# A two-layer transformer block: row-summing exponential on ScalarE, and the output projection's last two columns by token halves

## What is computed

```python
h = rms_norm(x, g[0]);  x = x + 0.5 * rms_norm(swiglu(h, w_ffn_in[layer, 0], w_ffn_out[layer, 0]), g[1])
h = rms_norm(x, g[2])
qa, ka, va, qh, fh, ih, gh = split(h @ w_in[layer])
ya = rms_norm(sliding_window_sink_attention(qa, ka, va, sinks, rel_bias), attn_out_gain)
yh = hgrn2_mixer(qh, fh, ih, gh, lower_bounds, hgrn_norm_gain)
x = x + rms_norm(concatenate([ya, yh]) @ w_out[layer], g[3])
h = rms_norm(x, g[4]);  x = x + 0.5 * rms_norm(swiglu(h, w_ffn_in[layer, 1], w_ffn_out[layer, 1]), g[5])
# in the attention, 8 heads, windows of 128 keys, one sink logit a head:
m = maximum(max(logits), sink);  p = exp(logits - m)
probs = p / (sum(p) + exp(sink - m))
```

## Time and profile before

| | |
|---|---|
| median of 3 runs | 1989.49 us |
| the profiled execution | 1988.35 us |
| its span | 1986.6 us |
| PE busy | 1926.0 us, 97% |
| DVE busy | 747.1 us, 38% |
| ACT busy | 676.0 us, 34% |
| POOL busy | 871.9 us, 44% |
| mean granted TensorE clock | 0.995 |

### The profile page before, as it was taken

One profiled execution on the slowest core, in us unless ns is written; L12 is line 12 of the kernel. 1 busy time (PEld: TensorE's weight loads), 2 busy tenths in 40 slices (PEclk: granted clock), 3 DMA queues, 4 the chain that ended last, 5 costly groups with the idle time before them and its releaser, 6 DMA issues.

```text
span 1986.6 us, 29215 instructions
## 1 busy us (share of the span) xinstructions
PE 1926.0 (97%) x11226; PEld 1581.1 (80%) x11226; DVE 747.1 (38%) x1118; ACT 676.0 (34%) x904; POOL 871.9 (44%) x407
## 2 busy tenths in 40 slices
PE   6999999999999999999999999999999999999998
PEld 5888888877777788888888888888777778888887
DVE  4322210377775522210162222105777663222103
ACT  4332322443444323232253232224333453323221
POOL 5444445442235544345363444455322354444452
PEclk9999999999999999999999999999999999999999
DMA  5323233221112232323322323232211223232331
GB/s 173 106 85 106 89 101 115 93 84 61 54 65 85 85 106 86 104 95 109 104 85 95 100 90 106 95 112 83 89 50 53 75 75 106 95 103 87 106 106 64
DMA packets 54040, 182.81 MB, mean 92 GB/s; under 512 B 6696, under 2 KB 10312, under 8 KB 53960
## 3 DMA queue, kind: packets, MB, share of 16 engines
q1 hardware_dynamic: 53960, 181.65, 28.0%
HBM read 179.14 MB, written 2.49 MB: 91 GB/s over the span
## 4 chain that ended last, share of the span: by engine, by line
PE 86%; DVE 5%; issue 3%; POOL 2%; POOLq 2%; ACT 1%; DVEq 1%; DMA 0%; SPq 0%; ACTq 0%
PE bank L685 25%; PE bank L687 24%; PE bank L686 24%; PE pair L825 2%; DVE SM L1184 2%; PE bank L703 2%; PE bank L704 2%; POOLq L378 1%; PE bank L711 1%; POOL WLO L369 1%; PE pair L685 1%; PE pair L686 1%; PE pair L687 1%; DVE TREE_F L1172 1%; DVE QE L1174 1%
## 5 line engine op out<-in xcount | busy, mean ns | idle before, releaser
L369 POOL TENSOR_TENSOR WLO<-RAW,WHI 128x1024 fp32r<-128x1024 f32 (+1 forms) x336 | 794.9, 2386 | 1062.3 <-ACT WHI L426 1061.8
L686 PE MATMUL bank<-HLO,WHI 128*128 128x512 f32 x1616 | 630.2, 390 | 0.0
L685 PE MATMUL bank<-HHI,WHI 128*128 128x512 f32 x1568 | 621.4, 396 | 2.0 <-DVE TMP L982 1.0
L687 PE MATMUL bank<-HHI,WLO 128*128 128x512 f32 x1568 | 611.4, 390 | 0.0
L426 ACT ACTIVATE WHI<-RAW 128x1024 fp32r<-128x1024 f32 (+1 forms) x336 | 337.0, 1037 | 73.5 <-PE bank L687 55.1
L686 PEld LDWEIGHTS bank<-HLO,WHI 128*128 128x128 f32 x1616 | 303.6, 188 | 60.8 <-issue 0.5
L685 PEld LDWEIGHTS bank<-HHI,WHI 128*128 128x128 f32 x1568 | 294.3, 188 | 68.8 <-issue 3.2
L687 PEld LDWEIGHTS bank<-HHI,WLO 128*128 128x128 f32 x1568 | 294.4, 188 | 62.2
L685 PE MATMUL bank<-UHI,WHI 128*128 128x512 f32 x616 | 242.9, 394 | 0.0
L687 PE MATMUL bank<-UHI,WLO 128*128 128x512 f32 x616 | 241.6, 392 | 0.0
L686 PE MATMUL bank<-ULO,WHI 128*128 128x512 f32 x616 | 239.2, 388 | 0.0
(11 more groups left out here) (183 smaller groups left out, 1843.4 us busy)
## 6 DMA issues: line engine op xcount, KB each, us to landing
RAW<-stream SPq DMA_DIRECT2D x336, 512.0 KB, 3.7
X<-xT SPq DMA_DIRECT2D x4, 512.0 KB, 9.0
yT<-X SPq DMA_DIRECT2D x16, 128.0 KB, 1.8
bias<-rel_scratch SPq DMA_DIRECT2D x4, 128.0 KB
rel_scratch<-SM SPq DMA_DIRECT2D x1, 382.0 KB
mask_sb<-masks SPq DMA_DIRECT2D x1, 256.0 KB, 10.7
par<-sinks SPq DMA_DIRECT2D x4, 2.0 KB, 4.3
par<-params SPq DMA_DIRECT2D x1, 60.0 KB, 2.2
```

Source lines behind the costliest of these rows:

```text
L369: pool.tensor_tensor(WLO[:, n, 0:cols], RAW[:, n, 0:cols], WHI[:, n, 0:cols], ALU.subtract)\
L685: pe.matmul(dst, WHI[:, slot, lhs], rhs_hi, start=first, stop=False)
L686: pe.matmul(dst, WHI[:, slot, lhs], rhs_lo, start=False, stop=False)
L687: ins = pe.matmul(dst, WLO[:, slot, lhs], rhs_hi, start=False, stop=last)
```

## The change

The softmax: DVE makes the negated maximum with one instruction (the sinks are negated once, in the setup) and the sinks' differences; it no longer subtracts over the logits nor sums the rows. ACT runs one exponential for each of the 8 blocks of 128 keys, with the negated maximum as its bias and the row sum as its second output, and one more for the sinks. `next_take(0)` moves from in front of the wait for the exponential to behind `p_ready`. The output projection: columns 6 and 7 both run by halves (banks 2 and 5 for the first halves, 3 and 6 for the second); SS holds six columns, and two squares are added at each end; ACT's order becomes `high` 0, split, square of column 6, `high` 1, 2, square of column 7, `high` 3, split, root. DVE copies the second half of column 6 in its pre stage, behind the batch of part 3. The semaphore counts change through `half_count`; the FFNs' own ends keep their order.

```diff
--- before.py
+++ after.py
@@ -99,6 +99,11 @@
 BATCHES = [[0], [1, 2], [3], [4], [5, 6], [7], [8, 9], [10], [11]]
 TEMPS = [(5, 0), (5, 1), (7, 1), (5, 0), (5, 1), (6, 1), (5, 0), (4, 0), 6, 5, 4, 6]
 LAST = 3 * DEPTH - 1
+
+
+def half_count(g):
+
+    return g + (g + 1) // 3
 
 
 def parts_of(g):
@@ -503,16 +508,40 @@
                             elif not (last and b == 3 and n >= per - (1 if g < LAST else 2)):
                                 split_hi(L, c0 + b * per + n + 2, i, 4 * per)
                         q = Q_POST[s] + b
-                        if not (last and b == 3):
+                        if not (last and b >= (2 if k_outer else 3)):
                             act.wait_ge(proj_free, L * LAYER_JOBS + i * 4 + (j0 + b + 1 + PROJ_BANKS))
                             act.wait_ge(sq_free, L * LAYER_SQ + i * 4 + (q + 1))
                             act.activation(SQ[:, q % 2, :], Y[:, i * 4 + b, :], ACT.Square).then_inc(sq_done, 1)
                 body(0, False)
                 body(1, True)
 
+                first, second = HALVES_OF
+                if k_outer:
+                    q = Q_POST[s] + KT - 2
+                    for n, b in enumerate((2, 5)):
+                        act.wait_ge(half_full, half_count(g) + n + 1)
+                        act.wait_ge(sq_free, L * LAYER_SQ + (q + n + 1))
+                        act.activation(SQ[:, (q + n) % 2, first], bank[b][:, 0:HALF], ACT.Square).then_inc(half_sq, 1)
+                    act.wait_ge(half_sum, g + 1)
+                    rsqrt_mean(bank[7][:, first], bank[4][:, 0:HALF], D_MODEL).then_inc(post_r, 1)
+
+                    def second_square(n, b):
+                        act.wait_ge(w_used, L * LAYER_CHUNKS + (c0 + KT - 2 + n + 1 + SPLIT_SLOTS))
+                        act.activation(SQ[:, (q + n) % 2, second], bank[b][:, 0:HALF], ACT.Square).then_inc(sq_done, 1)
+
+                    high(g + 1, 0)
+                    split_hi(L, c0 + KT + 1)
+                    second_square(0, 3)
+                    high(g + 1, 1)
+                    high(g + 1, 2)
+                    second_square(1, 6)
+                    high(g + 1, 3)
+                    split_hi(L, c0 + KT + 2)
+                    act.wait_ge(sq_free, L * LAYER_SQ + (q + 2 + SQ_SLOTS))
+                    rsqrt_mean(bank[7][:, second], bank[4][:, 0:HALF], D_MODEL).then_inc(post_r, 1)
+                    return
                 q = Q_POST[s] + KT - 1
-                first, second = HALVES_OF
-                act.wait_ge(half_full, g + 1)
+                act.wait_ge(half_full, half_count(g) + 1)
                 act.wait_ge(sq_free, L * LAYER_SQ + (q + 1))
                 act.activation(SQ[:, q % 2, first], bank[5][:, 0:HALF], ACT.Square).then_inc(half_sq, 1)
                 act.wait_ge(half_sum, g + 1)
@@ -606,7 +635,10 @@
                     if t > 0:
                         head_norm(t - 1)
                     act.wait_ge(logit_ready, it + 1)
-                    act.activation(S[:], S[:], ACT.Exp).then_inc(exp_ready, 1)
+                    for n in range(8):
+                        act.activation(Slog[:, n, :], Slog[:, n, :], ACT.Exp, bias=small[:, 0, n:n + 1],
+                                       accum_out=small[:, 1, n:n + 1])
+                    act.activation(Ssink, Ssink, ACT.Exp).then_inc(exp_ready, 1)
                     ahead(0)
                     for half in range(2):
                         act.wait_ge(pt_full, it * 2 + (half + 1))
@@ -735,6 +767,30 @@
                         total(SS[:], 4, (sq_free, L * LAYER_SQ + (Q_PRE[s] + KT + SQ_SLOTS)), pre_sum)
                 return at
 
+            def out_end(L, c, hi, lo, tiles):
+
+                g = L * 3 + 1
+                first, second = HALVES_OF
+                own = slice(0, HALF)
+                q = Q_POST[1] + KT - 2
+                for n, b in enumerate((2, 5)):
+                    chunk(L, c + n, tiles, hi, lo, b, signal=half_full, w=own, rhs_w=first)
+                pe.wait_ge(sq_free, L * LAYER_SQ + (q + SQ_SLOTS))
+                pe.matmul(bank[4][:, own], ones[:], SS[:, first], start=True, stop=False)
+                chunk(L, c, tiles[:3], hi, lo, 3, ready=False, done=False, w=own, rhs_w=second)
+                for n in range(2):
+                    pe.wait_ge(half_sq, half_count(g) + n + 1)
+                    ins = pe.matmul(bank[4][:, own], ones[:], SQ[:, (q + n) % 2, first], start=False, stop=n == 1)
+                ins.then_inc(half_sum, 1)
+                chunk(L, c, tiles[3:], hi, lo, 3, ready=False, w=own, rhs_w=second)
+                chunk(L, c + 1, tiles, hi, lo, 6, ready=False, w=own, rhs_w=second)
+                pe.wait_ge(post_r, 2 * g + 1)
+                pe.matmul(bank[4][:, own], ones[:], SS[:, second], start=True, stop=False)
+                for n in range(2):
+                    pe.wait_ge(sq_done, L * LAYER_SQ + (q + n + 1))
+                    ins = pe.matmul(bank[4][:, own], ones[:], SQ[:, (q + n) % 2, second], start=False, stop=n == 1)
+                ins.then_inc(sq_free, 2)
+
             def down(L, s, c0, j0, width, hi, lo, h=None, m0=0):
 
                 g = L * 3 + s
@@ -745,13 +801,17 @@
                 def tiles_of(n):
                     return [(k - n * TILES, k, k == 0, k == width - 1) for k in range(n * TILES, min(width, (n + 1) * TILES))]
 
-                for m in range(m0, KT - 1):
+                pair_end = s == 1
+                for m in range(m0, KT - 2 if pair_end else KT - 1):
                     bank_free(L, j0 + m)
                     for n in range(per):
                         wait = h is not None and m == 0
                         chunk(L, c0 + m * per + n, tiles_of(n), hi, lo, m % 4,
                               h_sem=h[0] if wait else None, h_value=h[1] if wait else None)
                 bank_free(L, j0 + KT - 1)
+                if pair_end:
+                    out_end(L, c0 + KT - 2, hi, lo, tiles_of(0))
+                    return
                 c_last = c0 + (KT - 1) * per
                 for n in range(per):
                     chunk(L, c_last + n, tiles_of(n), hi, lo, 5, done=n == per - 1, signal=half_full, w=own, rhs_w=first)
@@ -762,16 +822,13 @@
                     tiles = tiles_of(n)
                     if n == 0:
                         chunk(L, c_last, tiles[:3], hi, lo, 6, ready=False, done=False, w=own, rhs_w=second)
-                        pe.wait_ge(half_sq, g + 1)
+                        pe.wait_ge(half_sq, half_count(g) + 1)
                         pe.matmul(bank[4][:, own], ones[:], SQ[:, q % 2, first], start=False, stop=True).then_inc(half_sum, 1)
                         tiles = tiles[3:]
-                    if n == per - 1 and per > 1:
+                    if n == per - 1:
                         pe.wait_ge(post_r, 2 * g + 1)
                         pe.matmul(bank[4][:, own], ones[:], SS[:, second], start=True, stop=False)
                     chunk(L, c_last + n, tiles, hi, lo, 6, ready=False, w=own, rhs_w=second)
-                if per == 1:
-                    pe.wait_ge(post_r, 2 * g + 1)
-                    pe.matmul(bank[4][:, own], ones[:], SS[:, second], start=True, stop=False)
                 pe.wait_ge(sq_done, L * LAYER_SQ + (q + 1))
                 pe.matmul(bank[4][:, own], ones[:], SQ[:, q % 2, second], start=False, stop=True).then_inc(sq_free, 1)
 
@@ -1021,6 +1078,9 @@
                     for p in batch:
                         k, w = parts[p]
                         dve.tensor_tensor(X[:, k, w], X[:, k, w], temp(p), ALU.add).then_inc(x_ready, 1)
+                    if batch[-1] == SPLIT_TILES - 1 and s == 2:
+                        dve.wait_ge(sq_done, L * LAYER_SQ + (Q_POST[1] + KT - 1))
+                        dve.tensor_copy(Y[:, KT - 2, HALVES_OF[1]], bank[3][:, 0:HALF]).then_inc(proj_free, 1)
                     if batch[-1] == 2 * SPLIT_TILES - 2:
                         take_last()
                 gain = par[:, L, P_GAIN + 2 * s * KT:]
@@ -1033,12 +1093,16 @@
 
             def down(L, s, c0, j0, per, k_outer=False):
 
-                for m in range(KT - 1):
+                for m in range(KT - 2 if k_outer else KT - 1):
                     c = c0 + 3 if k_outer and m < 4 else c0 + m * per + per - 1
                     take(L, c, Y[:, m, :], bank[m % 4][:], scale=False,
                          four=(2, m) if k_outer and m < 4 else None).then_inc(proj_free, 1)
                     add_square(L, Q_POST[s], m)
-                dve.wait_ge(half_sq, L * 3 + (s + 1))
+                g = L * 3 + s
+                dve.wait_ge(half_sq, half_count(g) + 1)
+                if k_outer:
+                    dve.tensor_copy(Y[:, KT - 2, HALVES_OF[0]], bank[2][:, 0:HALF])
+                    dve.wait_ge(half_sq, half_count(g) + 2)
                 dve.tensor_copy(Y[:, KT - 1, HALVES_OF[0]], bank[5][:, 0:HALF])
                 dve.drain()
 
@@ -1143,23 +1207,19 @@
                     top = small[:, 0, :]
```

(11 more changed lines are left out.)

## The result

The changed kernel takes 1973.51 us (median of 4 runs, 1973.25 to 1973.74), the kernel before 1988.99 beside it: 15.5 us less, a ratio of 0.9923 with a 95% interval from 0.9911 to 0.9935. The forecast was 1980.3 with 1978.0 to 1986.0 as its range. The direction was right and the gain was taken too small by 6 to 7 us, outside the range. The profiled execution took 1973.74 us, its span 1971.7, at a granted clock of 0.998.

A forecast was written before the change was run, and what follows sets the result against it. TensorE, 97% busy, was taken to bound the kernel, with gains only where it stands still. Output projection 6.7 plus softmax 2.5 made 9.2 us off: 1979.15 for the profiled execution, 1980.3 as median, range 1978.0 to 1986.0.

The forecast's parts named there:

- What bounds the kernel: Whole kernel: TensorE is busy 97% of 1986.6 us, so only its stalls, at most some 60 us, can be won.
- Part 1: Output projection's end: running columns 6 and 7 by halves brings the second root earlier, 3.1 + 3.6 = 6.7 us.
- the stage hangs on the second root: Output projection: the stage's end moves with the second root, HLO ending 22.4 us behind it, not with TensorE's restart.
- (c): Output projection: second root stays behind in ACT's queue, so less is won; 1982.3 to 1984.5 us, chance 0.10.
- (d): Output projection: POOL's additions and HLO fall apart, HLO runs nearer its unheld time; 1976 to 1978.9 us, chance 0.05.
- Part 2: Softmax: shorter wait ahead of the transposes, 0.75 us in each of 2 first heads, 0.17 in 6 others, 2.5 us.
- floor of 0.35: Softmax's transposes: TensorE needs about 0.35 us to go over to small tiles even where nothing is late.
- The idle time as the price: Softmax's transposes: recorded idle time, 1.41 and 0.52 us, less 0.35 taken as winnable: 1.06 and 0.17 a head.
- The 0.3 that a first head was to lose: First head's softmax: WLO runs until 434.3 and holds `widen(0)`, needed by the scores at 434.73; 0.3 us lost.
- price X: Softmax on ACT: time of one 128-element exponential with its row sum, taken as 0.45 us, between 0.28 and 0.74.
- (a): Softmax: price X between 0.575 and 0.68 eats up to 6.7 us of Part 1; 1982.8 to 1989 us, chance 0.16.
- (b): Softmax: price X over 0.68, ACT's row-wise exponentials bound each head's transposes; 1993.4 us at 0.74, chance 0.08.

The follow-up runs named there:

- e13: Changed kernel with five 128-element copies on ACT ahead of the output projection's second root, their scratch tile declared behind all others; 1975.03 us.
- e2: Kernel before with only the output projection's end run by halves, softmax unchanged; 1980.67 us.
- e7: Changed kernel with the third weight split of the next FFN moved behind the second root on ACT; 1973.49 us.
- e1: Kernel before with only the softmax's edits, output projection's end unchanged; 1981.46 us.
- e12: Changed kernel with four more row exponentials on ACT in each head, their scratch tile declared behind all others; 1979.76 us.
- e4: Changed kernel with only `next_take(0)` put back in front of the wait for the exponential; 1980.41 us.
- e8: Changed kernel with one unused tile of 32 bytes a partition declared ahead of UHI and ULO, nothing else; 1982.22 us.
- e11: Changed kernel with one unused tile of 64 bytes declared ahead of UHI and ULO, nothing else; 1981.93 us.
- e5: Changed kernel with four more row exponentials on ACT in each head, 1296 bytes of scratch tiles declared ahead of UHI and ULO; 1988.54 us.
- e6: Changed kernel with five short copies on ACT ahead of the second root, 1296 bytes of scratch tiles declared ahead of UHI and ULO; 1983.91 us.
- e9: Changed kernel with four more row exponentials on ACT in each head, padding ahead of UHI and ULO made 1408 bytes; 1986.64 us.
- e10: Changed kernel with five short copies on ACT ahead of the second root, padding ahead of UHI and ULO made 1408 bytes; 1982.2 us.
- e14: Changed kernel with five small tiles taken from ahead of UHI and ULO, one unused 512-byte tile in their place; 1969.88 us.

## Why the prediction was wrong, step by step

**What bounds the kernel** was right: TensorE's stalls at these two places were the gain, and 97% busy hid both.

**Part 1, the output projection's end, 6.7 us:** right. Relative to the stretch ahead the second root came 3.09 and 3.54 us sooner (3.15 and 3.6 forecast), and root to last HLO stayed at 22.36. The step "the stage hangs on the second root" is borne out by e13 (the root 0.98 later, the layers 0.97 and 1.04 longer from root to root) and by e2 (the roots forecast at 622.24 and 628.6 were over at 622.35 and 628.60). e7 limits it: a root 0.33 sooner, with a split put behind it, brought nothing. TensorE's lead over the root became a wait for HLO of 1.1 us a layer, as said; the square of column 7 was not waited for at all. Rivals (c) and (d) did not come about.

**Part 2, the softmax, 2.5 us:** the mechanism was right, the size wrong by a factor of three; by the heads' marks it brought 1.5 in each first head and 0.7 to 0.8 in each other one, 7.5 us, and e1 gives 7.6 without part 1. Three terms of the sum failed.

- *The floor of 0.35.* "TensorE needs about 0.35 to go over to small tiles even where nothing is late" was read from the row of L864, but that row is the weight load's (PEld). TensorE's own row beside it has no idle time and starts 0.32 behind the matmul ahead, 0.09 more than their pace of 0.23 (kernel before, first head):

```profile
421.44 0.39 PE L687 MATMUL bank<-HHI,WLO 128*128 128x512 f32 x1
421.76 1.10 PE L864 MATMUL pair<-kT,PROJ 64*64 64x128 f32 x32
```

  In the changed kernel the transposes have no idle time on PE in any of the eight heads, where the forecast's sign was 0.35 in all. The floor was taken off all eight: 8 x 0.35 = 2.8 us.
- *The idle time as the price.* The page draws a matmul 0.39 long but starts the next one 0.23 behind it. A stall's cost is from start to start less 0.23, so the idle time shown falls short by 0.16: 8 x 0.16 = 1.3 us. Reading 432.99 to 434.79 would have shown 1.57 where I used 1.06.
- *The 0.3 that a first head was to lose* at `widen(0)` behind WLO. The hold is there (L1233 takes 0.83 for 0.41, and WLO takes 3.03), but the second half of `widen(0)` is over at 434.56 (434.15 + 0.41) and the scores start at 434.62, 1.01 behind the transposes, where it was 0.99 before: 2 x 0.3 = 0.6 us. That WLO would be held until the product's end, on which the 0.3 rested, no row of the kernel before shows. In the changed kernel WLO starts at 430.91, 0.47 behind the product, and is over at 433.94; 434.3 was forecast.

Together 4.7 of the missing 5.0. The price X of a row was forecast at 0.45 and is 0.385, the overlapped pair (0.38) of the forecast's own list. It mattered little: at 0.45 a first head would have been 8 x 0.06 = 0.5 us late, and a later one has 1.06 of slack. Rivals (a) and (b) did not come, since X is far from their point of 0.575; that point was close (in a first head 0.39 + 1.50 / 8 = 0.58). e12 stands near it, with 1.54 us of rows more: its first head reaches the mark 75.02 us behind the root against 75.06 before (461.77 - 386.75 and 461.93 - 386.87), and the later heads' 39.04 is near the 39.2 of before. The row with its sum shows as two instructions on ACT, ACTIVATE and ACTIVATION_READ_ACCUMULATOR at 0.19.

What was not forecast is that moving `next_take(0)` carries the gain. I costed it at nothing, and that is right for what waits for the take, but wrong for what the take makes late: e4 loses 6.9 us with it back in its place, of the 7.5. The order in which DVE's product and POOL's WLO start is decided by it.

**About 1.0 us more, in neither part:** from the last HLO to the next stage's first root the kernel before takes 336.41 and 336.71, the changed one 336.04 twice, and e2 336.04 twice. In the trace of before, TensorE, which ran at a granted clock of 0.57 from 630 to 634, reaches the next norm's sum later (its root R is over 0.09 us ahead of the last HLO's end; 1.18 in the changed kernel), and DVE's gate product, beside a WLO, then takes 2.46 us against 1.90 in the changed kernel (layer 0; its next one takes 0.69). That chain is read from traces and wasn't tried by itself. e1, which keeps the old end, has 337.26 in layer 0 but 336.04 in layer 1, so more than the stall decides it.

The sum by the runs: 6.6 + 7.5 + 1.0 = 15.1 us, less 0.4 by which the changed kernel's profiled execution started later (its first wait for a DMA took 11.1 us, in the kernel before 10.7), which leaves 14.7, against 14.6 between the two profiled executions (1988.35 and 1973.74).

## What to carry to other kernels

Price a stall from start to start of the waiting engine's instructions, less their undisturbed pace, and take a floor only from that engine's own rows and from the same kind of instruction with nothing late; the idle time on the page is a lower bound. Here the page had 1.41 for 1.57 and e12's 0.40 for 0.56. When an instruction is moved past others, ask which of two instructions that were seen to hold each other now starts first (DVE's product and POOL's WLO here: 2.99 us for 1.23 or 3.03 for 2.39), not only who waits for its result. And before a slope is measured by adding work, look where its scratch tile is declared: declare it last (e12 and e13 kept the 0.2289 us a matmul), or run the tile alone first (e8: 8.7 us for 32 unused bytes).

## What the runs showed of the hardware

The matmuls of 512 columns that read UHI and ULO follow each other at a pace that changed with the tiles declared ahead of these two. Averaged over 400 steps from 265 us on it was 0.2289 us in the kernel before and in the changed kernel, and 0.2333, 2% more, with 32 (e8), 64 (e11), 1296 (e5 and e6) or 1408 bytes (e9 and e10) a partition added ahead. With the added tiles declared last it was 0.2289 (e12, e13), and in e14, with five small tiles moved from ahead of them behind and an unused tile of 512 bytes in their place, 0.2267. No trace holds an address, and no run shows what lies behind these paces. That it is the place of the tiles in SBUF, and their offset against 2048 bytes, is my estimate from the sizes alone; e14 is one arrangement only.

In the changed kernel (L639) the row sum on ACT is read out by an instruction of 0.19 us of its own, and the next row starts 0.09 us behind the read-out's start (427.00 and 426.91): an exponential of 128 elements with its row sum takes 0.39 us in all.
